# Latent keys of layer 1 made token by token, a later weight split in the pair slots, and six early rows with a ring of seven in layer 0's output

## What is computed

```python
def _rmsnorm(x, g):
    y = xf * lax.rsqrt(jnp.mean(xf * xf, axis=-1, keepdims=True) + EPS)
    return (y * g.astype(F32)).astype(x.dtype)

def _mla_kv(mkv, mkr, ckv_g, wukv, mk_g, rope):
    kv = (_rmsnorm(mkv, ckv_g) @ wukv).reshape(B, L, M_HEADS, NOPE_DIM + V_DIM)
    k_n = _rmsnorm(kv[..., :NOPE_DIM], mk_g[:NOPE_DIM])
    ...
    return k, kv[..., NOPE_DIM:]

h_lat = h_lat + g_l * (o_lat @ w_out[i])
h_ctx = h_ctx + g_c * (o_ctx @ w_out[i])
```

## Time and profile before

| | us |
|---|---|
| median of 3 runs | 1544.5 (1544.37 to 1548.87) |
| the profiled execution's own time | 1547.81 |
| its span | 1546.0 |
| TensorE busy | 1480.4 (96%) |
| VectorE busy | 1025.7 (66%) |
| ScalarE busy | 576.3 (37%) |
| GpSimd busy | 216.9 (14%) |
| layer 0's output, first tile | about 819.8 to 841.2 |
| layer 1, slots 19 to 40 | about 1217.0 to 1444.4 |

### The profile page before, as it was taken

The page is one execution under the profiler, slowest core; times in us unless marked ns, Lnnn a source line. Parts: engine busy times, 40 slices in busy tenths (PEclk is TensorE's granted clock), DMA queues, the critical chain, the costliest instruction groups (busy, mean ns, idle before and its releaser), DMA issues.

```text
span 1546.0 us, 19313 instructions
## 1 busy us (share of the span) xinstructions
PE 1480.4 (96%) x7755; PEld 1178.5 (76%) x7755; DVE 1025.7 (66%) x1199; ACT 576.3 (37%) x806; POOL 216.9 (14%) x242
## 2 busy tenths in 40 slices
PE   5999999999999999999998999989999888999998
PEld 1336888888888787778885888867888775788998
DVE  3384998889897776867774545465576555665543
ACT  2553222222223334333333111162366555655332
POOL 1001332323330100000000344420000000000000
PEclk9999999999999999999999999989999999999999
DMA  9998455545454644453557566422333231233563
GB/s 353 385 367 334 164 193 171 193 138 194 160 166 161 231 137 146 147 207 134 188 212 262 196 227 207 158 91 101 109 109 110 75 103 48 75 110 134 186 224 139
DMA packets 72904, 272.29 MB, mean 176 GB/s; under 512 B 11056, under 2 KB 25584, under 8 KB 53104
## 3 DMA queue, kind: packets, MB, share of 16 engines
q1 hardware_dynamic: 52640, 193.45, 35.4%
q0 software_dynamic: 20176, 77.61, 14.6%
HBM read 256.36 MB, written 14.68 MB: 175 GB/s over the span
## 4 chain that ended last, share of the span: by engine, by line
PE 87%; DMA 5%; DVE 3%; ACT 3%; issue 2%; POOL 0%; SPq 0%; ACTq 0%; DVEq 0%; POOLq 0%
PE banks L1025 22%; PE banks L1026 22%; PE banks L1029 22%; DMA ada_ring<-in_ada_first 2%; PE banks L1195 2%; PE banks L1182 2%; PE banks L2109 2%; PE banks L2039 1%; PE banks L1278 1%; DMA hybias<-in_hy_bias 1%; PE banks L538 1%; DVE rs L2274 1%; PE banks L1246 1%; PE banks L999 1%; PE banks L2099 1%
## 5 line engine op out<-in xcount | busy, mean ns | idle before, releaser
L1025 PE MATMUL banks<-xh,wh 128*128 128x512 f32 (+1 forms) x1808 | 618.0, 357 | 0.6 <-ACT wh L977 0.6
L1026 PE MATMUL banks<-xl,wh 128*128 128x512 f32 (+1 forms) x1808 | 603.0, 349 | 0.0
L1025 PEld LDWEIGHTS banks<-xh,wh 128*128 128x128 f32 x1808 | 341.8, 189 | 52.4 <-issue 7.8
L1026 PEld LDWEIGHTS banks<-xl,wh 128*128 128x128 f32 x1808 | 342.0, 189 | 46.0 <-issue 3.1
L1029 PE MATMUL banks<-xh,wl 128*128 128x512 f32 (+1 forms) x1808 | 354.9, 349 | 0.0
L1029 PEld LDWEIGHTS banks<-xh,wl 128*128 128x128 f32 x1808 | 295.9, 189 | 43.7
L987 DVE TENSOR_TENSOR wl<-raw,wh 128x2048 fp32r<-128x2048 f32 (+1 forms) x124 | 281.2, 2268 | 58.4 <-ACT wh L977 58.4
L977 ACT ACTIVATE wh<-raw 128x2048 fp32r<-128x2048 f32 (+1 forms) x124 | 235.6, 1900 | 179.0 <-PE banks L1029 170.1
L373 DVE SCALAR_TENSOR_TENSOR ada_acc<-ada_w,cond,ada_acc 128x1024 f32<-128x1024 f32 x120 | 159.6, 1330 | 5.4 <-DMA ada_w<-in_ada_rest 3.2
L396 POOL DMA_DIRECT2D ada_w<-in_ada_rest x128 | 69.3, 541 | 559.2 <-DVE ada_acc L385 381.4
L385 DVE SCALAR_TENSOR_TENSOR ada_acc<-ada_w,cond,ada_acc 128x1024 f32<-128x1024 f32 x90 | 125.3, 1393 | 0.0
(11 more groups left out here) (293 smaller groups left out, 1622.2 us busy)
## 6 DMA issues: line engine op xcount, KB each, us to landing
ada_w<-in_ada_rest POOLq DMA_DIRECT2D x128, 512.0 KB, 3.8
raw<-in_ev_tiles SPq DMA_DIRECT2D x52, 1024.0 KB, 6.5
raw<-in_od_tiles SPq DMA_DIRECT2D x34, 1024.0 KB, 4.8
ada_ring<-in_ada_first SPq DMA_DIRECT2D x32, 1024.0 KB, 12.0
raw<-in_out_tiles SPq DMA_DIRECT2D x32, 1024.0 KB, 5.2
hT<-in_hT POOLq DMA_DIRECT2D x4, 1024.0 KB, 11.9
spectra<-kstage POOLq DMA_DIRECT2D x4, 1024.0 KB, 10.3
kf<-spectra SPq DMA_DIRECT2D x8, 512.0 KB, 5.4
```

Of the source, the lines that this page charges most:

```text
L1025: nc.tensor.matmul(out, wh[:, k, :], b.xh[:, seg, k, :], start=(k == 0), stop=False)
L1026: nc.tensor.matmul(out, wh[:, k, :], b.xl[:, seg, k, :], start=False, stop=False)
```

## The change

**Keys.** `kn` fills become `kt` fills: the same six matmuls, with 128 tokens stationary and the weights of 4 heads moving, as `vm` has it. A token's key is now along the row. ScalarE copies the fill into `ktok` and squares it into `sqk`; VectorE sums the squares along the row (`key_squares`), ScalarE takes one root of 128x16 (`key_roots`), VectorE one reciprocal of 128x16 and four products with a broadcast factor (`scale_keys`). In the gate slot after the key slot TensorE turns 16 blocks of 128x128 (`turn_keys`), and ScalarE copies them out of banks 4 to 7 with the gain (`keep_keys`, four instructions for each half). The 8 key `sums` and the 8 `pick` matmuls are gone.

**Places.** The key slots are 19 and 21, the pair slots 24, 26, 28 and 30 (`MLA_AT`); the units of MLA stand in 27, 28, 29, 30, 31, 33, 35 and 36. There are 41 slots as before, with 16 gates.

**The split in pair slots.** ScalarE does `split_high` of the next tile after the drain of the first fill, not ahead of it.

**Layer 0's output.** Rows 0 to 5 are loaded early, the ring has 7 slots at separate places, rows 6 to 9 are issued before the second tile's weights and 10 to 15 behind them.

```diff
-ORING = 6
+ORING = 7
...
-    b.orow = put("orow", "S", 28 * K, [P, ORING, T])
+    b.orow = [put(f"orow{n}", "S", at * K, [P, T]) for n, at in enumerate((28, 30, 32, 12, 0, 2, 34))]
...
+    b.ktok = [b.kn[:, 4 + t, :] for t in range(4)]
+    b.sqk = [put(f"sqk{n}", "U", at * K, [P, 512]) for n, at in enumerate((58, 62))]
+    b.kss = put("kss", "V", 2432, [P, 16])
+    b.krk = put("krk", "V", 2496, [P, 16])
...
-                for k in range(3):
+                for k in range(6):
                     load_o(sp, b, s, g, k)
...
-            for k in range(3, KT):
-                if k == ORING:
+            for k in range(6, KT):
+                if k == 10:
                     load_raw(sp, b, s, t0 + 1, out_weights(g, 0, 1), (KT, P))
                 if k >= ORING:
                     sp.wait_ge(s.out_o_low, k - ORING + 1)
...
-MLA0 = 19
-NORMED = ("ckv", "kr", "k", "q", "cq", "kn", "qn", "qr")
-PICK_LAG = 6
+MLA_AT = {19: ("k", 0), 21: ("k", 1), 24: ("q", 0), 26: ("q", 1), 28: ("q", 2), 30: ("q", 3)}
+KEY_TURN = {20: 0, 22: 1}
+NORMED = ("ckv", "kr", "k", "q", "cq", "qn", "qr")
 ROTATED = ("kr", "k", "q", "qr")
-GROUPED = {"ckv": 2, "cq": 4, "kn": 4}
+GROUPED = {"ckv": 2, "cq": 4}
...
+    if i in MLA_AT:
+        side, n = MLA_AT[i]
+        if side == "k":
+            return [("kt", 4 * n + t, T) for t in range(4)] + [("vm", 4 * n + t, T) for t in range(4)]
+        return [("qn", 2 * n, 256), ("qn", 2 * n + 1, 256), ("qr", n, 256)]
...
-MLA_SLOTS = (24, 25, 26, 28, 30, 32, 34, 36)
+MLA_SLOTS = (27, 28, 29, 30, 31, 33, 35, 36)
...
-            if kind in ("kn", "vm"):
+            if kind in ("kt", "vm"):
...
-                        if kind == "kn":
-                            lhs, rhs, out = w[wp][:, k, 256 * (n % 4):256 * (n % 4) + P], xp[:, k, :], bank
-                        else:
-                            lhs = xp[:, k, P * (n % 4):P * (n % 4) + P]
-                            rhs = w[wp][:, k, :].rearrange("p (h c) -> p h c", h=4)[:, :, P:2 * P]
-                            out = bank.rearrange("p (h c) -> p h c", h=4)
+                        lhs = xp[:, k, P * (n % 4):P * (n % 4) + P]
+                        side = slice(0, P) if kind == "kt" else slice(P, 2 * P)
+                        rhs = w[wp][:, k, :].rearrange("p (h c) -> p h c", h=4)[:, :, side]
+                        out = bank.rearrange("p (h c) -> p h c", h=4)
...
                 if swaps_before(m + 1):
                     pe.wait_ge(s.odd_swap_used, swaps_before(m + 1))
-                if count_fills(m - 1, ("kn",)):
-                    last = max(j for j in range(m) if fill_is(j, ("kn",)))
-                    pe.wait_ge(s.odd_normed, count_fills(last, NORMED))
-            lhs = {"kr": b.blocks64, "qr": b.blocks64, "kn": b.batch[:, 112 - 16 * (n % 4):240 - 16 * (n % 4)]}
+                if kind == "qn":
...
-        def pick(m):
-
-            n = FILLS[m][1]
-            last = m + 3 - n % 4
-            pe.wait_ge(s.odd_rstd, count_norms(last))
-            if n % 4:
-                pe.wait_ge(s.odd_normed, count_fills(m - 1, NORMED))
-            nc.tensor.matmul(ps[7], b.pick[:, n % 4, :], b.rs1[:], start=True, stop=True).then_inc(s.odd_pick, 1)
+        def turn_keys(half):
+
+            if half == 0:
+                pe.wait_ge(s.odd_out, 8)
+                pe.wait_ge(s.odd_probT, 8)
+                pe.wait_ge(s.odd_root, count_norms(FIRST_FILL[min(MLA_AT)] - 1))
+                pe.wait_ge(s.odd_swap_used, swaps_before(FIRST_FILL[min(MLA_AT)]))
+            else:
+                pe.wait_ge(s.odd_kread, 6)
+            for t in range(4):
+                pe.wait_ge(s.odd_kmade, 9 * half + 6 + t)
+                for h in range(4):
+                    last = nc.tensor.transpose(ps[4 + t][:, P * h:P * h + P], b.ktok[t][:, P * h:P * h + P], b.ident)
+                last.then_inc(s.odd_kturned, 1)
...
+            if i in KEY_TURN:
+                turn_keys(KEY_TURN[i])
...
+            if kind == "kt":
+                half, t = divmod(n, 4)
+                if half:
+                    act.wait_ge(s.odd_kturned, t + 1)
+                a.activation(b.ktok[t], bank, ACT.Copy).then_inc(s.odd_kcopied, 1)
+                if n > 1:
+                    act.wait_ge(s.odd_kmade, 9 * half + t - 1 if t > 1 else 3 + t)
+                a.activation(b.sqk[t % 2][:], bank, ACT.Square).then_inc(s.odd_drained, 1)
+                return
...
+        def key_roots(half):
+            act.wait_ge(s.odd_kmade, 9 * half + 4)
+            a.activation(b.krk[:], b.kss[:], ACT.Sqrt, scale=1.0 / 128, bias=b.small[:, 0:1]).then_inc(s.odd_kread, 1)
+
+        def keep_keys(half):
+            for t in range(4):
+                act.wait_ge(s.odd_kturned, 4 * half + (4 if half else t + 1))
+                a.activation(b.kn[:, 4 * half:4 * half + 4, P * t:P * t + P],
+                             ps[4 + t].rearrange("p (h t) -> p h t", h=4), ACT.Copy,
+                             scale=b.cols[:, COL["mk_n"]:COL["mk_n"] + 1]).then_inc(s.odd_kread, 1)
...
+            pair_slot = l1_slot(i)[0][0] == "qn"
+            if i > 1 and not pair_slot:
                 split_high(nc, act, b, s, t0 + i + 1, width(i + 1))
+            if KEY_TURN.get(i - 1) == 1:
+                keep_keys(1)
             for m in range(FIRST_FILL[i], FIRST_FILL[i + 1]):
                 gate_slot = FILLS[m][0] == "gate"
                 if gate_slot and closes_norm(m - 1):
                     root(m - 1)
                 drain(m)
+                if pair_slot and m == FIRST_FILL[i]:
+                    split_high(nc, act, b, s, t0 + i + 1, width(i + 1))
                 if not gate_slot and closes_norm(m - 1):
                     root(m - 1)
+                if fill_is(m - 2, ("kt",)) and FILLS[m - 2][1] % 4 == 3:
+                    key_roots(FILLS[m - 2][1] // 4)
...
+            if KEY_TURN.get(i - 1) == 0:
+                keep_keys(0)
...
-        def scale_kn(m):
-            n = FILLS[m][1]
-            dve.wait_ge(s.odd_pick, n + 1)
-            dve.wait_ge(s.odd_kept, count_fills(m, NORMED))
-            v.scalar_tensor_tensor(out=b.kn[:, n, :], in0=b.kn[:, n, :], scalar=b.cols[:, COL["mk_n"]:COL["mk_n"] + 1],
-                                   in1=ps[7], op0=ALU.mult, op1=ALU.mult).then_inc(s.odd_normed, 1)
+        def key_squares(m):
+            half, t = divmod(FILLS[m][1], 4)
+            dve.wait_ge(s.odd_drained, m + 1)
+            if half and t == 0:
+                dve.wait_ge(s.odd_kread, 1)
+            v.tensor_reduce(b.kss[:, 4 * t:4 * t + 4], b.sqk[t % 2][:].rearrange("p (h c) -> p h c", h=4), AX.X,
+                            ALU.add).then_inc(s.odd_kmade, 1)
+
+        def scale_keys(half):
+            dve.wait_ge(s.odd_kread, (1, 2)[half])
+            v.reciprocal(b.krk[:], b.krk[:]).then_inc(s.odd_kmade, 1)
+            dve.wait_ge(s.odd_kmade, 9 * half + 5)
+            dve.wait_ge(s.odd_kcopied, 4 * half + 4)
+            for t in range(4):
+                x = b.ktok[t].rearrange("p (h c) -> p h c", h=4)
+                v.tensor_tensor(x, x, b.krk[:, 4 * t:4 * t + 4].unsqueeze(2).to_broadcast([P, 4, P]),
+                                ALU.mult).then_inc(s.odd_kmade, 1)
...
-                if fill_is(m - PICK_LAG, ("kn",)) and not group_end(m - PICK_LAG):
-                    scale_kn(m - PICK_LAG)
+                if fill_is(m - 1, ("kt",)):
+                    key_squares(m - 1)
+                if fill_is(m - 3, ("kt",)) and FILLS[m - 3][1] % 4 == 3:
+                    scale_keys(FILLS[m - 3][1] // 4)
```

More of the change, by code:

```diff
@@ L1682, in load_o @@
         sp.wait_ge(s.gated_out[k % 2], 16 * ((k - HEADS) // 2 + 1))
-    sp.dma_start(b.orow[:, k % ORING, :], g.o_d[k]).then_inc(s.out_o_in[k % ORING], 16)
+    sp.dma_start(b.orow[k % ORING][:], g.o_d[k]).then_inc(s.out_o_in[k % ORING], 16)
 OUT_TILES = KT
@@ L1850, in l1_slot @@
         return [("cq", i - 15, 256)]
[L1851 to L1856, removed]
+    if i in MLA_AT:
[3 more added lines that the diff above has]
+        return [("qn", 2 * n, 256), ("qn", 2 * n + 1, 256), ("qr", n, 256)]
     return [("gate", l1_gate(i), 256)]
 def l1_gate(i):
-    if i >= MLA0 + 12:
-        return i - MLA0 - 6 if i < L1_TILES else None
-    return (i - MLA0) // 2 if i > MLA0 and (i - MLA0) % 2 else None
+    if i < min(MLA_AT) or i in MLA_AT or i >= L1_TILES:
+        return None
+    return i - min(MLA_AT) - sum(at < i for at in MLA_AT)
 FILLS = [f for i in range(L1_TILES) for f in l1_slot(i)]
@@ L1893, in swap_step @@
     return m + (1 if FILLS[m][0] == "qr" else 2)
-def group_end(m):
-    return fill_is(m, ("kn",)) and FILLS[m][1] % 4 == 3
 def hurried(m):
@@ L2074, in scores @@
                 pe.wait_ge(s.odd_kr, 1)
+                pe.wait_ge(s.odd_kread, 10)
             if u > 0:
@@ L2115, in _ @@
                     fill(i, m)
-                if fill_is(m - PICK_LAG, ("kn",)) and not group_end(m - PICK_LAG):
-                    pick(m - PICK_LAG)
                 for r in rotated_at(m):
```

(13 more changed lines are left out.)

16 lines of the change are left out of this document (6 added, 10 removed).

## The result

The changed kernel takes 1528.22 us (median of 4 runs, 1527.16 to 1529.77); the kernel before took 1546.41 beside it (4 runs, 1544.37 to 1548.87). The ratio is 0.9888, with a 95% interval of 0.9876 to 0.9900: faster by 1.1%. The profiled execution took 1527.92 us against 1547.81, 19.9 less. The forecast of 1528.0 lies 0.2 us from the median, and that closeness is luck. For the profiled execution I had 1531.3 us, and it took 1527.92, so 3.4 us more were won than forecast. The two errors cancelled. By the medians taken beside one another 18.2 us were won, where I had 16.5. The mechanism has to be judged by the rows.

The account below looks back on a forecast made before the run. TensorE was taken to bound the kernel (87% of the span). Terms -10.7 - 2.6 + 0 - 3.2 = -16.5 us took the profiled 1547.81 to 1531.3; less 3.3 us of profile above median, 1528.0 us, range 1521 to 1536.5.

Parts of the forecast that it names:

- TensorE bounds, and its work counts in full: Layer 1: 16 sums and picks go (13.9 us), 32 turned blocks come (3.2 us); net -10.7 us, all on TensorE without cover.
- Waits of layer 1: From slot 19 on, TensorE's waits would total 16.7 us against 19.3: -2.6 us, ends -6 to +2.
- in 28 and 30 the second sum waits for the root: Pair slots 28 and 30: the second head's sums wait for ScalarE's root, some 2.3 us each, 0.1 ahead of a sum.
- Falls of the clock: Layer 1: four drops to 1.2 GHz behind waits, as before: 0 us, one or two either way at 1.6 us each.
- the slower rival: Slots 19 to 24: the array stays at 1.2 GHz, costing up to 45 us; at 27 us the time is 1555. Chance 0.03.
- Moving the split gains nothing: Pair slots: an earlier first drain, but the same five ScalarE steps end at the same root; first sum's gain returns at second.
- keep_keys, the broadcast products and the four table loads are covered: Layer 1: this added ScalarE and VectorE work lies beside gate fills or idle time; uncovered, `keep_keys` would cost up to 5 us.
- Layer 0's output: First tile of layer 0's output: `xh` rows and second tile's `wh` come earlier, -3.2 us; ends 2.1 and 4.2 us.
- turned blocks leave the clock at 1.00: Rival for slots 21 and 23: turned blocks leave the array at 1.2 GHz, 1531.2 us, or 1532.2 with dearer blocks. Chance 0.05.
- VectorE is no bound: Rival for the key slots: VectorE's reductions and products become the bound, +6.5 us, giving 1534.5. Chance 0.12.
- The early rows do give something: Rival for layer 0's output: early rows give nothing since the weights' megabyte sets the first tile's end, 1531.2 us. Chance 0.10.
- The rival of more to be won: No falls behind shorter waits (slots 28, 30, layer 0) and 2 us fewer waits: 1521.5 us. Chance 0.12.

Follow-up runs that it names:

- e7_rotate_early: The changed kernel with the rotation of `qr` moved into the softmax of the same slot in slots 27, 29 and 31: 1526.09 us.
- e3_split_first: The changed kernel with the split of the next tile back at the start of the pair slots: 1524.21 us, ratio 0.9861.
- e1_out_only: The kernel before with only the change's part in layer 0's output: 1543.7 us against 1545.46, ratio 0.9991 (unclear by the runs).
- e8_cq_later: The changed kernel with the `cq` root moved beside the keys' root and the rest of its normalisation into slot 20: 1520.62 us, ratio 0.9841.
- e2_keys_only: The changed kernel without its part in layer 0's output (old ring of six, three early rows): 1531.34 us, ratio 0.9913.

## Why the prediction was right, point by point

- *TensorE bounds, and its work counts in full.* Right. Sums and picks less turned blocks: forecast -10.7; measured 13.9 - 3.3 = -10.6, of which only the 3.3 was timed anew. As a remainder it comes out too: 228.3 less 19.3 of waits and 6.8 of clock is 202.2, 211.7 less 14.9 and 5.1 is 191.7, so -10.5.
- *Waits of layer 1*: one of two terms that were mis-sized. Forecast 16.7 for 19.3, measured 14.9, so 1.8 us more were won. Slot 19: 5.0 for 5.7. Slot 24 1.6 (1.6), slot 25 2.9 (2.9), slot 26 1.4 (1.2). Slot 27: 0.1 (0.6). Slots 28 and 30: 1.8 and 2.1 (2.3 and 2.4). The step "in 28 and 30 the second sum waits for the root" named the wrong wait: the first sum waits for the rotation on bank 7. e7_rotate_early showed that the forecast one stands just behind it, which is why the size came out nearly right.
- *Falls of the clock*: the other term that was mis-sized. I took four for four, 0 us. The change has three: of the waits in 28 and 30, about 2 us each, only one was followed by a fall. That is 1.7 us. Work 10.6, waits 4.4 and clock 1.7 make 16.7, against the 16.6 measured; the forecast had 13.3. I also wrote that every fall in the trace of before was over after about 4 us. That was misread: one about 1010 us, between the layers, lasts 10.2 us, so the chance of the slower rival rested on a wrong premise.
- *Moving the split gains nothing*: right in slots 28 and 30. In 24 and 26 it does not only give back what it takes, it costs 1.5 us of waits (e3_split_first).
- *keep_keys, the broadcast products and the four table loads are covered*: right; the key slots show no wait for VectorE, whose reductions take 0.68 us and whose products 0.69.
- *Layer 0's output*: forecast -3.2; -3.5 in the change's first tile, -3.1 in e1_out_only.
- *The rivals*: turned blocks leave the clock at 1.00, so that one is out. VectorE is no bound. The early rows do give something (1.3 us). The rival of more to be won came in part: 1.8 us fewer waits than forecast (it had 2), and of its falls one. The slower one did not come.

## What to carry to other kernels

Price matmuls that only sum or spread a vector by their pass over the columns: here a 512-column fp32 one costs 0.87 us, and summing along the row on an engine with room and turning 128x128 blocks at 0.10 us is cheaper. Ahead of moving a step, list every semaphore of the instruction that waits, and the time at which each is met: in pair slots 28 and 30 three chains end within 2 us of one another, and moving one or two of them gave nothing there. And look for work whose result nobody needs yet in front of the drain that holds the array: moving `cq`'s normalisation out of slot 19 was worth 6.5 us for a few lines.

## What the runs showed of the hardware that I had not expected

The same wait is not always followed by the same clock. Kernel before and e1_out_only have the same twelve waits in layer 1 to 0.03 us, and lose 6.8 and 5.1 us to the clock. In the change the 1.8 us wait of slot 28 was followed by a fall and the 2.0 us wait of slot 30 was not (the windows above); in e9_change_again, the same kernel, it was the other way round:

```profile
1306.40:1310.40 4.00, 3.78 (x25) 3.37 (x26) 3.90 (x4) 2.79 (x6) 0.00 (x0) 1.00 0.20 29
1330.20:1334.20 4.00, 3.95 (x17) 3.70 (x18) 3.90 (x4) 2.85 (x6) 0.00 (x0) 0.62 0.12 20
```

Nine traces have both of these waits: seven have a fall behind one of them, two (e3_split_first, e8_cq_later) behind neither, and none behind both. I had forecast one behind each. From slot 19 on a fall lasts 3.4 us and costs 1.7, or lasts 6.8 and costs 3.4; e2_keys_only has such a long one behind the 3.2 us wait of slot 19, and none behind the wait of slot 25. So a difference of about 2 us between two single traces of different code can be one fall, however equal the waits; the clock column has to be read beside it.
